# A two-block network on one core: tanh gates and a new order in the recurrent mixer, x on a second DMA queue, low parts spread over the attention heads

## What is computed

```python
def rglru_mixer(h, ...):                      # layer 0, h = rms_norm(x)
    gate, xr = jnp.split(h @ w_in, 2, axis=-1)
    gate = jax.nn.gelu(gate)
    xc = conv of xr with 4 causal taps + conv_b
    r = jax.nn.sigmoid(xb @ w_a + b_a)        # xb: 4 blocks of 256 channels
    i = jax.nn.sigmoid(xb @ w_x + b_x)
    log_a = -RG_C * r * softplus(-lam)        # RG_C = 8
    a = jnp.exp(log_a)
    u = jnp.sqrt(-jnp.expm1(2.0 * log_a)) * (i * xc)
    hs = scan of hs[t] = a[t] * hs[t-1] + u[t]
    return (hs * gate) @ w_out
```

## Time and profile before

| | |
|---|---|
| runs | 865.27, 865.31, 871.66 us; median 865.31 |
| profiled execution | 869.99 us, of which the span 868.2 |
| TensorE matmul busy | 854.7 us (98%), 7192 records |
| VectorE busy | 653.5 us (75%) |
| ScalarE busy | 497.7 us (57%) |
| mixer | to 77.2 us, its output products to 102.1 |
| attention | 278.8 to about 387 us |
| granted TensorE clock, mean | 0.994 |

### The profile page before, as it was taken

The page is one execution under the profiler, slowest core; times in us unless marked ns, Lnnn a source line. Parts: engine busy times, 40 slices in busy tenths (PEclk is TensorE's granted clock), DMA queues, the critical chain, the costliest instruction groups (busy, mean ns, idle before and its releaser), DMA issues.

```text
span 868.2 us, 17572 instructions
## 1 busy us (share of the span) xinstructions
PE 854.7 (98%) x7192; PEld 833.9 (96%) x7192; DVE 653.5 (75%) x1245; ACT 497.7 (57%) x907; POOL 44.4 (5%) x62
## 2 busy tenths in 40 slices
PE   8999999999999999999999999999999999999998
PEld 7978999999999898899999999999999999999998
DVE  6768668888977696576667555576699899997873
ACT  5686687774335566567878444444446555445550
POOL 0000000000000125200000000022020000000000
PEclk9999999999999998999999999999999999999999
DMA  9906787788878724148766865635554422565541
GB/s 302 342 9 218 247 260 232 266 272 290 285 251 255 250 81 144 49 147 268 214 186 174 258 199 195 194 98 125 192 193 149 138 82 74 164 201 183 178 150 49
DMA packets 162817, 164.23 MB, mean 189 GB/s; under 512 B 16768, under 2 KB 159280, under 8 KB 162480
## 3 DMA queue, kind: packets, MB, share of 16 engines
q1 hardware_dynamic: 162736, 163.10, 59.4%
HBM read 162.01 MB, written 2.91 MB: 190 GB/s over the span
## 4 chain that ended last, share of the span: by engine, by line
PE 79%; DVE 9%; ACT 4%; DMA 3%; SPq 2%; issue 2%; POOL 1%; DVEq 0%
PE ps L316 20%; PE ps L320 20%; PE ps L318 20%; DVE wl L283 3%; DMA aw<-in_w_adaT_dram 2%; PE ps L1551 2%; PE ps L1553 2%; PE ps L1549 2%; PE ps L1610 2%; DMA raw<-in_rec_w_in_dram 1%; PE ps L1645 1%; PE ps L1647 1%; PE ps L1649 1%; SPq L2223 1%; DVE aw L843 1%
## 5 line engine op out<-in xcount | busy, mean ns | idle before, releaser
L283 DVE TENSOR_TENSOR wl<-raw,wh 128x1024 fp32r<-128x1024 f32 x256 | 308.8, 1223 | 28.8 <-ACT wh L276 28.7
L316 PE MATMUL ps<-xh,wh 128*128 128x256 f32 x1136 | 320.0, 282 | 0.1
L318 PE MATMUL ps<-xl,wh 128*128 128x256 f32 x1136 | 315.4, 278 | 0.3
L320 PE MATMUL ps<-xh,wl 128*128 128x256 f32 x1136 | 315.4, 278 | 0.0
L276 ACT ACTIVATE wh<-raw 128x1024 fp32r<-128x1024 f32 x256 | 266.8, 1051 | 69.8 <-PE ps L320 61.3
L316 PEld LDWEIGHTS ps<-xh,wh 128*128 128x128 f32 x1136 | 214.4, 189 | 2.4 <-issue 1.0
L318 PEld LDWEIGHTS ps<-xl,wh 128*128 128x128 f32 x1136 | 214.2, 189 | 0.8 <-DVE xl L384 0.7
L320 PEld LDWEIGHTS ps<-xh,wl 128*128 128x128 f32 x1136 | 213.9, 188 | 0.0
L320 PE MATMUL ps<-hh,wl 128*128 128x256 f32 x512 | 141.4, 276 | 0.5 <-DVE wl L283 0.5
L318 PE MATMUL ps<-hl,wh 128*128 128x256 f32 x512 | 141.3, 276 | 0.0
L316 PE MATMUL ps<-hh,wh 128*128 128x256 f32 x512 | 141.3, 276 | 0.0
(11 more groups left out here) (359 smaller groups left out, 1419.2 us busy)
## 6 DMA issues: line engine op xcount, KB each, us to landing
raw<-in_w_in_dram SPq DMA_DIRECT2D x34, 1024.0 KB, 5.3
raw<-in_mlp_up_dram SPq DMA_DIRECT2D x32, 1024.0 KB, 5.4
raw<-in_mlp_down_dram SPq DMA_DIRECT2D x32, 1024.0 KB, 7.1
aw<-in_w_adaT_dram SPq DMA_DIRECT2D x24, 512.0 KB, 4.9
raw<-in_rec_w_in_dram SPq DMA_DIRECT2D x7, 1024.0 KB, 11.3
raw<-in_att_w_in_dram SPq DMA_DIRECT2D x6, 1024.0 KB, 6.1
raw<-in_rec_w_out_dram SPq DMA_DIRECT2D x4, 1024.0 KB, 6.3
raw<-in_att_w_o_dram SPq DMA_DIRECT2D x4, 1024.0 KB, 5.0
```

What stands on the lines that cost most here:

```text
L283: e.tensor_tensor(parts_of(i)[1], raw_of(i), f32(parts_of(i)[0]), op=ALU.subtract).then_inc(S["wl"], 1)
L316: e.matmul(o, H[:, first + n], xh[:, k], start=start and n == 0, stop=False)
L318: e.matmul(o, H[:, first + n], xl[:, k], start=False, stop=False)
L320: ins = e.matmul(o, L[:, first + n], xh[:, k], start=False, stop=stop and n == len(ks) - 1)
```

## The change

- Gates: sigmoid(z) is computed as (1 + tanh(z/2))/2. GpSimd halves the two biases once (`bh`). The factors 1/2 go into the decay constants (8 becomes 4, with a bias added), into the square root (scale 0.25) and into the input gate (`(ii + 1) * xc`).
- Decays: each pair of tiles gets its exponentials and squares right behind its gates (`scalar_decays`), not all eight behind the last block; VectorE's v follows pair by pair.
- Order in the mixer: gate1 moves between blocks 2 and 3; VectorE's taps stand earlier, low parts one at a time.
- Output products: ro0 and ro1 begin with y tiles 0 to 5 each and take tiles 6 and 7 afterwards.
- Loads: ScalarE issues the four loads of x; SyncE loads the first weight chunk in four pieces with a semaphore each.
- Norms: in both MLPs the spread stands behind up2 (the context's behind up17), in the attention behind c and not kw.
- Attention: each step k = 0 to 7 makes one low part (step 0 made four, steps 1, 3, 5 one each). The last two steps' values go to AUX banks; wo0 and wo1 go on, and wo2 is begun, beside the last heads.

```diff
@@ tensor_whole
-        q.wait_ge(S[f"raw{c % NRAW}"], 16 * (c // NRAW + 1))
         for k in range(8):
+            if c == 0 and k < 6:
+                q.wait_ge(S[f"first{k // 2}"], 16)
+            else:
+                q.wait_ge(S[f"raw{c % NRAW}"], 16 * (c // NRAW + 1))
@@ tensor_mixer
-        tensor_x(e, q, "gate0", (S["gl"], 1))
-        tensor_block(e, q, 2)
-        tensor_block(e, q, 3)
-        for f in range(1, 8):
+        for n in (2, 3):
+            tensor_x(e, q, f"gate{n - 2}", (S["gl"], n - 1))
+            tensor_block(e, q, n)
+        for f in range(2, 8):
             tensor_x(e, q, f"gate{f}", (S["gl"], f + 1))
@@ vector_input_gate
-            e.tensor_tensor(II[:, t], II[:, t], XC[:, t], op=ALU.mult).then_inc(S["ig"], 1)
+            e.scalar_tensor_tensor(II[:, t], II[:, t], 1.0, XC[:, t], op0=ALU.add, op1=ALU.mult).then_inc(S["ig"], 1)
@@ vector_mixer, the new middle, from the third low part on
         vector_decay_c(e, q)
+        lows(e, q, 4)
+        vector_xr(e, q, 3)
+        vector_xr(e, q, 4)
+        vector_taps(e, q, 2)
         lows(e, q, 5)
+        vector_taps(e, q, 3)
         lows(e, q, 6)
         vector_xr(e, q, 5)
         vector_taps(e, q, 4)
         vector_xr(e, q, 6)
+        vector_input_gate(e, q, 0)
         vector_taps(e, q, 5)
+        vector_xr(e, q, 7)
+        lows(e, q, 7)
+        vector_taps(e, q, 6)
+        vector_v(e, q, 0)
+        vector_v(e, q, 1)
+        vector_taps(e, q, 7)
         vector_input_gate(e, q, 1)
+        vector_gate(e, q, 0)
+        lows(e, q, 8)
+        vector_v(e, q, 2)
+        vector_v(e, q, 3)
         lows(e, q, 9)
         vector_input_gate(e, q, 2)
+        vector_gate(e, q, 1)
+        vector_v(e, q, 4)
+        vector_v(e, q, 5)
         lows(e, q, 11)
         vector_input_gate(e, q, 3)
         lows(e, q, 12)
+        vector_v(e, q, 6)
+        vector_v(e, q, 7)
+        vector_gate(e, q, 2)
@@ scalar_gates, scalar_decays
+        q.wait_ge(S["bh"], 1)
-            e.activation(RR[:, t], ps[f"ri{t}.0"], ACT.Sigmoid, bias=vc("b_a", t)).then_inc(S["sg"], 1)
+            e.activation(RR[:, t], ps[f"ri{t}.0"], ACT.Tanh, scale=0.5, bias=vc("b_a", t)).then_inc(S["sg"], 1)
...
-            e.activation(TH[:, t], RR[:, t], ACT.Tanh, scale=cpos[:, t:t + 1]).then_inc(S["th"], 1)
+            e.activation(TH[:, t], RR[:, t], ACT.Tanh, scale=cpos[:, t:t + 1], bias=cpos[:, t:t + 1]).then_inc(
+                S["th"], 1)
+    def scalar_decays(e, q, n):
+        for t in (2 * n, 2 * n + 1):
+            scalar_decay(e, q, t)
+        for t in (2 * n, 2 * n + 1):
+            scalar_decay_square(e, q, t)
@@ scalar_mixer, the new middle
+        scalar_load(e)
...
         scalar_xc(e, q, 3)
+        scalar_xc(e, q, 4)
+        scalar_gates(e, q, 0)
         highs(e, q, 6)
+        scalar_decays(e, q, 0)
+        scalar_xc(e, q, 5)
+        scalar_xc(e, q, 6)
+        highs(e, q, 7)
+        scalar_xc(e, q, 7)
         highs(e, q, 8)
         scalar_gates(e, q, 1)
+        scalar_decays(e, q, 1)
         highs(e, q, 9)
         scalar_gates(e, q, 2)
+        scalar_decays(e, q, 2)
         highs(e, q, 11)
         scalar_gates(e, q, 3)
+        scalar_decays(e, q, 3)
         highs(e, q, 12)
@@ tensor_ro
-        for f in range(8):
-            o = main(q, (S["x"], f + 1))[:, 0:256]
-            product(e, q, f"ro{f}", o, YH, YL, lambda k: (S["yh"], k + 1), lambda k: (S["yl"], k + 1))
+        for lo, hi in ((0, 6), (6, 8)):
+            for f in range(2):
+                tensor_ro_part(e, q, f, lo, hi)
+        for f in range(2, 8):
+            tensor_ro_part(e, q, f, 0, 8)
@@ tensor_mlp
-            if f == 1:
+            if f == 2:
                 rms_spread_pe(e, q, 1 + 2 * l)
@@ tensor_latent
         tensor_x2(e, q, "kw", (S["ki"], 2), (S["wt"], 1))
+        tensor_x2(e, q, "c", (S["c"], 1))
         rms_spread_pe(e, q, 2)
-        tensor_x2(e, q, "c", (S["c"], 1))
@@ tensor_values, tensor_outputs
-        p = claim(q, AUX[0], (S["os"], 8)) if m == 7 else main(q, (S["os"], m + 1))
+        p = claim(q, AUX[m - 6], (S["os"], m + 1)) if m > 5 else main(q, (S["os"], m + 1))
...
-        p = claim(q, AUX[1], (S["ol"], 8)) if m == 7 else main(q, (S["ol"], m + 1))
+        p = claim(q, AUX[0], (S["ol"], 8)) if m == 7 else main(q, (S["ol"], m + 1))
@@ tensor_attention
+            if k == 9:
+                tensor_wo(e, q, 0, 5, 7)
+                tensor_wo(e, q, 1, 6, 7)
             if k > 1:
                 tensor_outputs(e, q, k - 2)
...
-        tensor_wo(e, q, 0, 5, 8)
-        tensor_wo(e, q, 1, 6, 8)
-        for f in range(2, 8):
+        tensor_wo(e, q, 2, 0, 7)
+        for f in range(3):
+            tensor_wo(e, q, f, 7, 8)
+        for f in range(3, 8):
             tensor_wo(e, q, f, 0, 8)
@@ vector_attention
-            if k == 0:
-                for m in (1, 2, 3):
-                    lows(e, q, ahead(f"q{m}")[1])
-                    if m > 1:
-                        vector_q(e, q, m)
             if k > 1:
                 vector_outputs(e, q, k - 2)
+            if k < 8:
+                lows(e, q, at["q5"] + k + 1)
+            if k == 0:
+                vector_q(e, q, 2)
+                vector_q(e, q, 3)
             for n, step in enumerate(QSTEPS):
-                if step == k and n % 2 == 0:
-                    lows(e, q, ahead(f"q{4 + n // 2}")[1])
                 if step == k and n % 2:
                     vector_q(e, q, 4 + n // 2)
@@ sync_all
-        sync_chunks(e, q, 0, 1)
+        sync_first(e, 0)
         e.dma_start(VEC[:], vec[:]).then_inc(S["vec"], 16)
-        for i in range(4):
-            e.dma_start(X[:, 2 * i:2 * i + 2], xv[:, 2 * i:2 * i + 2]).then_inc(S[f"x{i}"], 16)
+        for i in (1, 2, 3):
+            sync_first(e, i)
         sync_chunks(e, q, 1, 2)
@@ gpsimd
+            q.wait_ge(S["vec"], 16)
+            e.tensor_scalar(vc("b_a", 0, 16), vc("b_a", 0, 16), 0.5, None, op0=ALU.mult).then_inc(S["bh"], 1)
```

More of the change, by code:

```diff
@@ L1304, in scalar_latent @@
         highs(e, q, ahead("qi3")[0])
+        scalar_qi(e, q, 3)
         highs(e, q, ahead("kw")[0])
+        q.wait_ge(S["mm"], done["kw"])
+        e.activation(WT[64:72, :], ps["kw"][64:72], ACT.Copy).then_inc(S["wt"], 1)
+        highs(e, q, ahead("c")[0])
         q.wait_ge(S["mm"], done["spread2"])
```

112 lines of the change are left out of this document (50 added, 62 removed), and 2 rows, old and new, of the table S.

## The result

The changed kernel takes 859.63 us (median of 8 runs, 857.79 to 861.60), the kernel before 867.48 us on the same chip (8 runs, 865.27 to 873.23). The ratio, taken over all runs and not from the two medians, is 0.9901, with a 95% interval of 0.9879 to 0.9922. The forecast was 853.5 us, in a range of 849 to 859. On the three runs it started from, the ratio gives 865.31 x 0.9901 = 856.7 us, inside the range; the plain median of 859.63 is 0.6 us above it. The profiled execution takes 859.15 us (span 857.3) against 869.99, which is 10.8 us less where the sum said 14.0.

The account below looks back on a forecast made before the run. The prediction took TensorE as the bound, busy 854.7 of 868.2 us. Its terms, 0.3 + 4.6 + 1.8 + 0.9 + 5.2 + 1.2 = 14.0 us, gave 865.31 - 14.0 + 2.2 = 853.5 us, range 849 to 859.

Parts of the forecast that it names:

- four places of the earlier trace: Slow windows before: the mixer's blocks, the output products' start, attention step 2, behind the last heads; the change touches all four.
- Part 1: Start of the kernel: x from ScalarE's queue lets its last piece land sooner; gain 0.3 us, bounds 0 and 1.3.
- part 2: Mixer's middle: earlier taps and gate1 between blocks 2 and 3 let TensorE run on; gain 4.6 us, 1.7 of it clock.
- part 3: Start of the mixer's output products: the wait for y goes; gain 1.8 us.
- The tables: Mixer gates, a rival: tanh and exponential might need eight table loads between them, giving 858 us; chance 0.03.
- Part 4: Norms: spreads a product later cover TensorE's wait for GpSimd's power; gain 0.9 us (0.6 to 1.2).
- Part 5: Attention: one low part a step removes the flip's wait and step 2's low clock; gain 5.2 us, 2.8 of it clock.
- The rival on the slower side: Attention: a low part in each step delays the values and steps fall to the low clock; 875 us, slower chance 0.05.
- Part 6: Behind the last heads: wo0, wo1 and wo2 records cover waits; gain 1.2 us (0.9 to 1.4).
- half of the 4.5 us of low clock: Profile to median: unsure whether unprofiled runs have the mixer's and attention's low clock, the forecast adds back 2.2 us; chance 0.3.
- the clock stretches aren't in the median: Rival: unprofiled runs lack the low-clock stretches in mixer and attention, so only 9.5 us is gained, 855.8 us; chance 0.25.
- VectorE as the mixer's last chain: Rival at the mixer's output products: u begins 2.5 us or more late, TensorE waits for y again; 857.0 us, chance 0.08.

Follow-up runs that it names:

- e4: The changed kernel with SyncE again loading x and the first weight chunk in one piece: 861.74 us (one run).
- e0: The kernel before, unedited, run again: 867.71 us (12 runs), ratio 1.0013; its profiled execution takes 865.54 us at a mean clock of 0.998.
- e9: The kernel before with only the attention's change of one low part in each step: 862.11 us (10 runs), ratio 0.9949.
- e6: The changed kernel with gate1 again behind block 3 on TensorE, VectorE's and ScalarE's lists as changed: 860.87 us (one run).
- e7: The changed kernel with ro0 and ro1 whole again, not in two parts: 858.95 us (one run).
- e5: The changed kernel with the gates as sigmoids again, with the old constants, the new order kept: 867.58 us (10 runs), ratio 1.0026.
- e11: The changed kernel with the spreads of both MLPs behind up1 again: 860.1 us (one run).
- e8: The kernel of e3 with order and banks behind the last heads as in the kernel before: 857.32 us (one run).
- e1: The changed kernel with order and banks behind the last heads as in the kernel before: 857.0 us (4 runs), ratio 0.9884.
- e2: The changed kernel with three slices of wo2, not seven, ahead of the last slices of wo0 and wo1: 857.86 us (one run).
- e3: The changed kernel with each low part behind the residual addition in the attention's output products: 854.61 us (6 runs), ratio 0.9859.

## Why the prediction was right in sign and in five of six parts, and wrong in one

**What bounds the kernel:** right as to the gain. 13.5 of the 15.3 us came from the four places of the earlier trace rows, the rest from the start, the attention's norm and a stray wait. The loss came from a fifth place that those windows leave out.

**Part 1,** 0.3 forecast, 0.5 measured in place and 0.4 by e4: right, and for its reason. The first product moved 1.53 us and the sum 0.54, as far as the last piece of x: its `xg` starts at 8.46 us where the last two started at 9.01. VectorE:

```profile
8.46 0.62 DVE L564 TENSOR_SCALAR xg<-x,sb_vec 128x256 f32<-128x256 f32 x2 [0.59 <-DMA x<-in_xT_dram]
8.99 3.59 DVE L360 TENSOR_TENSOR sqa<-sqa,sqb 128x256 f32<-128x256 f32 x7
```

The sum's start in e4 and in the changed kernel, 13.05 and 12.64 us, differ by 0.4. What came earlier was the issuing. The issues of x, in the kernel before and in the changed one:

```profile
1.84 1.97 SPq L2239 DMA_DIRECT2D x<-in_xT_dram  x4
```
```profile
0.73 2.06 ACTq L693 DMA_DIRECT2D x<-in_xT_dram  x4
```

The last of the four begins at 2.30 us and not at 3.34; its transfer then takes 6.1 us and not 5.6, so it lands 0.5 us earlier.

**Parts 2 and 3,** 4.6 + 1.8 = 6.4 forecast, 7.0 - 0.5 = 6.5 measured against the profile that the prediction read. The fixed points held: taps 7 ends at 42.55 us (forecast 43.2), u begins at 58.64 (59.5), ro0's first record stands at 72.17 (72.7), the last low part of y at 74.6 to 75.0 and tile 7 wanted by 76.9. VectorE:

```profile
41.03 1.52 DVE L523 SCALAR_TENSOR_TENSOR xc<-xrp,sb_vec,xc 128x256 f32<-128x256 f32 x3
```
```profile
58.64 0.75 DVE L544 TENSOR_TENSOR ii<-ii,xrp 128x256 f32<-128x256 f32 x2
```
```profile
74.61 0.43 DVE L558 TENSOR_TENSOR yl<-gl,yh 128x256 fp32r<-128x256 f32 x1 [0.48 <-ACT yh L687]
```

Each has its forecast size too: ro0 begins 77.24 - 72.17 = 5.1 us earlier, which is 4.5 for part 2, and part 3 adds 1.9 by record 450. But part 2's size is that of one execution. In e0's profile ro0 begins at 74.62 us, and against it part 2 is worth 1.3 us and part 3 again 1.9; in e9's, with the same mixer, part 2 is worth 2.2. Of the 3.2 us between 4.5 and 1.3, 1.4 are shorter waits for the taps and the rest is the clock. Two edits to which the text gave a role had little or none: gate1's place (e6) and the two-part start of ro0 and ro1 (e7, 0.2 us). The tables, a rival with a chance of 0.03, did not come: the trace has two loads fewer. e5 shows how far the change leans on this: 7.2 us by the output products.

**Part 4,** 0.9 forecast; the attention's norm brought 0.56 in place and a later one 0.4, 1.0 in all. The size was right and a place wrong. The wait of the earlier trace rows is that of the context's norm, whose spread stands behind up17 now; the text called it the second MLP's. The MLPs' own spreads had nothing to give (e11).

**Part 5,** 5.2 forecast, 5.3 measured in place, and 0.5 more behind the last heads, which the text didn't see. The flip's wait is gone (2.2), and so is the step at a clock of 0.57 (3.0, for which the text has 2.8 in one place and 3.1 in another). The runs say a little less: 4.4 us by e9's ratio, 2.9 by its median. In e0's profile the stretch at a low clock is the shorter one (0.94 in the window of 330 to 338 us, against 0.57 in the first profile), and part 5 is worth 3.9 us against it. The rival on the slower side, that a low part in each step would delay the values, fell: step 1 takes 4.3 us, steps 2 to 6 take 4.6.

**Part 6 is the step that failed.** "The new step is that wo3 takes wo0's bank and must wait for the residual addition [...] 0 to 0.2 us" and "Gain 1.2 (0.9 to 1.4)". TensorE shows no wait for the bank, and the wait removed was worth its price: 1.7 us in place up to record 2865, 1.3 by e8. But I looked for the new wait only at the next user of the bank, and not at who waits for the additions in a row. 21 matmuls of wo2 ahead of wo0's last slice delay the first residual addition, against the last values' end, by 1.55 us (e1), and behind it stands a chain of eight tiles that is no faster than TensorE (2.87 against 2.72 or 2.83 us a tile) and ends in the second MLP's first product. So what decided was not TensorE's idle time at all: with or without it, up0 waits for the last addition. Part 6 is -1.5 us by e1, where the sum had +1.2; the table's 12.46 - 13.54 = -1.1 holds the 0.5 of part 5 as well. The last row ends at 369.14 us; no row of mine was of the stretch from there to the MLP, where the 0.58 us waits of VectorE stood in each tile.

**The sum again.** 0.5 + 6.5 + 1.0 + 5.3 - 1.1 = 12.2 us for the parts, against 14.0; the stretch of part 6 is 2.3 short (1.2 + 1.1), and the others are 0.5 above. The stray wait adds 0.7 and the two stretches of another pace take 1.4 and 0.7: 10.8, as profiled.

**From profile to median.** The forecast took half of the 4.5 us of low clock out of the gain. e0 bears that out in part: there the flip's wait had its low clock and the blocks' had not. But the waits at the blocks were shorter too, so that in place e0 is 4.3 us behind the changed kernel at record 450, not 7.0, 8.0 at 2700, not 13.5, and 6.4 at the end, not 10.85. The profile that the sum was read from was the worse of the two in all of this, and no term of the sum allows for it. The mean clock of 0.994 that the sum started from was met in 3 of 29 runs. At 0.998, the changed kernel's four runs have a mean of 859.5 us against the median of 866.5 in e0's batch: 7.0 us. The forecast with none of the clock was 9.5, and 9.5 less the 2.3 of part 6 is 7.2. So the rival "the clock stretches aren't in the median" was partly right. That the two sums agree so well is partly luck, since low clock was not wholly absent from the runs at 0.998 (e0's profile is one). The changed kernel also makes a place of its own for the clock to fall, behind up0's wait: 1.00 in its own profile, 0.72 or 0.50 in those of e2, e4, e6, e7 and e11, which cost 1.2 to 2.7 us up to record 3060. In e3, which has no such wait, all six runs have a clock of 1.000 and lie within 1.4 us of one another.

**VectorE as the mixer's last chain** (0.08) did not come: 41 records start without a gap from 72.17 us on.

**The best version is e3:** 854.61 us, 1.4% under the kernel before. In place it gains 4.2 us on the changed one behind record 3000 and ends 3.7 ahead. Of the 4.2, 1.3 are pace, and may be this execution's alone. Against the kernel before, the median is 11.7 us lower (866.29 - 854.61).

## What to carry to other kernels

When work is put ahead of a product's last piece, ask not only who takes the bank but who consumes the product: if its consumers form a chain that is no faster per tile than TensorE, then all of the delay reaches the end of that chain, here 20 us later and in the next layer. Set the chain's time a tile beside TensorE's time a product (2.87 against 2.72 to 2.83 us), and look inside the chain for a wait on the other engine that an independent operation could fill, before any reordering of matmuls. And take several executions' clock before counting a stretch at a low clock as a gain; where two profiles differ by a few us, count records in windows without a wait before looking for a cause in the edit.

## What was not expected of the hardware

- TensorE has two paces at a clock of 1.00, 0.1133 and 0.1178 us a record in products of the same shape. A stretch keeps its own, and two executions of one kernel differ in which one it is (e0). Over the 1544 records of the first MLP it cost e5's profile 6.5 us. That is enough to explain why runs of equal mean clock differ by 2 us and more (e9's six at 1.000 lie from 858.92 to 862.32 us), but only the profiled executions show their pace. What chooses the pace stays open.
- Behind the same waits of one kernel the mean clock varied from 0.994 to 1.000 between runs.
- A wait of 0.68 us for a low part stands near 256 us, late in the first MLP, in the first profile of the kernel before, and one of 0.65 at 249 us in e8's. e3's has 0.26 at the same matmul, the other traces nothing. It is in the 15.3 us above and belongs to no part of the change. In the first profile of before, VectorE sat idle for 3.13 us until 254.76, waiting for a load of `aw` (`w_adaT`), made an operation on it, and only then the low part, from 255.91 on, that TensorE took up at 257.18; in e8's it had waited 1.98 us for such a load. So a late load ahead of the low part in VectorE's list is what the traces show in front of it.
